# A hybrid decoder step on one core: value products one page at a time, probability turns two pages later, gate weights from ScalarE's queue, 4 key and 5 value page buffers, a combine step spread between gate products

## The reference

```
z = rmsnorm(x) @ w_in                       # q, k, v of two attentions, two gates
o_fox = softmax(q k^T/8 + c_q - c_k) v      # forgetting attention; samples: 2048 past keys in 16 pages
o_dil = sum_g softmax_g(lse_g) * o_g        # three dilated windows, mixed by their log-sum-exp
y = (sigmoid(gate_fox)*(o_fox @ w_br_fox) + sigmoid(gate_dil)*(o_dil @ w_br_dil)) @ w_mix_out
x = x + y ; then cross attention into 256 memory rows ; then a gated MLP with a convolution
```

## Time and profile before

| | us |
|---|---|
| median of 3 runs | 3113.7 (3109.15 to 3117.74) |
| the profiled execution | 3115.95 |
| its span | 3114.1 |
| PE busy | 2959.3 (95%) |
| DVE busy | 848.8 (27%) |
| ACT busy | 565.3 (18%) |
| mean granted clock of PE | 0.972 |

### The profile page before, as it was taken

One profiled execution on the slowest core, in us unless ns is written; L12 is line 12 of the kernel. 1 busy time (PEld: TensorE's weight loads), 2 busy tenths in 40 slices (PEclk: granted clock), 3 DMA queues, 4 the chain that ended last, 5 costly groups with the idle time before them and its releaser, 6 DMA issues.

```text
span 3114.1 us, 35981 instructions
## 1 busy us (share of the span) xinstructions
PE 2959.3 (95%) x13892; PEld 1862.2 (60%) x13892; DVE 848.8 (27%) x2145; ACT 565.3 (18%) x1247; POOL 135.3 (4%) x251
## 2 busy tenths in 40 slices
PE   8999999999789888889899999999999999999998
PEld 6655556776435444456544566446666666678887
DVE  2154543222532222223221023332222222210002
ACT  2233222212101111111100111322212212210001
POOL 0000001011001111000000000000000000000000
PEclk9999999999969999999999999999999999999999
DMA  4000111010136657545501301323433431121101
GB/s 170 20 11 8 52 45 53 11 47 15 30 105 174 199 159 206 181 155 163 204 27 54 135 28 48 128 66 116 146 118 120 152 118 42 29 86 38 38 1 58
DMA packets 195295, 276.95 MB, mean 89 GB/s; under 512 B 19741, under 2 KB 135406, under 8 KB 194086
## 3 DMA queue, kind: packets, MB, share of 16 engines
q1 hardware_dynamic: 177302, 210.83, 21.4%
q10 hardware_dynamic: 1504, 44.29, 3.7%
q0 software_dynamic: 16320, 19.52, 2.4%
HBM read 255.09 MB, written 58.90 MB: 101 GB/s over the span
## 4 chain that ended last, share of the span: by engine, by line
PE 82%; SPq 8%; DMA 4%; issue 3%; DVE 2%; ACT 0%; POOL 0%; DVEq 0%; POOLq 0%; ACTq 0%
PE psum L2240 21%; PE psum L2384 11%; PE psum L920 10%; PE psum L1870 8%; PE psum L1785 6%; PE psum L2005 4%; SPq L1399 3%; PE psum L677 3%; PE psum L693 3%; PE psum L1220 2%; DMA arena<-in_cache_fox_kv 2%; PE psum L1793 2%; PE psum L507 2%; PE psum L1236 2%; PE psum L1979 2%
## 5 line engine op out<-in xcount | busy, mean ns | idle before, releaser
L2240 PE MATMUL psum<-arena 128*128 128x288 f32 (+1 forms) x2112 | 645.9, 469 | 0.0
L2240 PEld LDWEIGHTS psum<-arena 128*128 128x128 f32 x2112 | 402.0, 190 | 243.5 <-issue 169.6
L2384 PE MATMUL psum<-arena 128*128 128x256 f32 (+1 forms) x1584 | 345.5, 381 | 0.7 <-DMA arena<-in_w_down 0.7
L920 PE MATMUL psum<-arena 128*128 128x512 f32 (+3 forms) x864 | 332.3, 515 | 1.4 <-ACT arena L560 1.4
L2384 PEld LDWEIGHTS psum<-arena 128*128 128x128 f32 (+1 forms) x1584 | 292.2, 185 | 53.5 <-issue 3.6
L1785 PE MATMUL psum<-arena 128*128 128x368 f32 (+1 forms) x768 | 310.8, 501 | 0.0
L1870 PE MATMUL psum<-arena 128*128 128x512 f32 (+1 forms) x576 | 266.0, 598 | 0.8 <-issue 0.8
L920 PEld LDWEIGHTS psum<-arena 128*128 128x128 f32 (+1 forms) x864 | 195.5, 262 | 70.2 <-issue 42.1
L1220 PEld LDWEIGHTS psum<-arena 128*128 128x128 f32 x848 | 107.4, 145 | 109.4 <-DMA arena<-in_cache_fox_kv 47.9
L1220 PE MATMUL psum<-arena 128*128 128x128 f32 x848 | 134.1, 282 | 35.7 <-DMA arena<-in_cache_fox_kv 35.2
L1785 PEld LDWEIGHTS psum<-arena 128*128 128x128 f32 x768 | 124.6, 195 | 63.6 <-issue 44.1
(11 more groups left out here) (207 smaller groups left out, 2630.7 us busy)
## 6 DMA issues: line engine op xcount, KB each, us to landing
arena<-in_cache_fox_kv SPq DMA_DIRECT2D x256, 256.0 KB, 3.1
out_win_s<-in_cache_win_kv ACTq DMA_DIRECT2D x8, 4080.0 KB, 15.3
arena<-in_w_up SPq DMA_DIRECT2D x44, 512.0 KB, 4.5
arena<-in_cache_win_kv SPq DMA_DIRECT2D x16, 1024.0 KB, 6.9
arena<-in_cache_mem_kv SPq DMA_DIRECT2D x16, 1024.0 KB, 6.0
arena<-in_w_down SPq DMA_DIRECT2D x4, 2816.0 KB, 9.9
arena<-in_w_in SPq DMA_DIRECT2D x9, 1024.0 KB, 7.8
arena<-in_x_prompt SPq DMA_DIRECT2D x16, 512.0 KB, 6.6
```

The lines of the kernel that those rows point to most:

```text
L920: last = pe.matmul(banks[c0 // 512][0:r, 0:cw], xn_tile(k, g, t), wD[g][:, k, c0:c0 + cw], start=(k == 0), stop=(k == KD - 1))
L2240: last = pe.matmul(banks[(u % 2) * 4 + x][:, 0:cw], wu[u % 3][:, k, :], xnT[:, k, c0:c0 + cw], start=(k == 0), stop=(k == KD - 1))
L2384: last = pe.matmul(banks[u % 2][0:r, 0:256], hT(f)[:, t * P:t * P + r], wd[q % 2][:, f, :], start=(f == 0), stop=(f == NF - 1))
```

## The change

Five things are changed; what is computed stays the same.

1. The schedule of the page attention is written with explicit offsets: the P of a sample come 2 to 6 pages into the next sample (before: 0, 2, 3, 4, 5), each V is one page (16 parts instead of 9; the last takes the new tokens too) at offsets 4 to 18, and O comes at 20. A V waits only for the group of probabilities that it reads, and P is copied as soon as the V that reads its old content is done.
2. Nine page buffers are split 4 for keys and 5 for values (before 3 and 6).
3. The gate weights are issued by ACT (`gates_load_act`) instead of SP, into two buffers instead of three.
4. In `PLAN`, `combine` has 84 units instead of 34, with more points at which gate products can stand between its pieces; `fox` has 360 (before 300), `dil` 192 (125), and `gb` 438 (258).
5. The window attention's mask and its 24 small loads of new keys are issued a quarter into `fox` (`dilprep_sp`), and the memory norm stands 14 units after the start of `mix`.

```diff
-    combine=(778, 812), ga=(715, 1010), gb=(1010, 1268), foxprep=(767, 777), fox=(814, 1114), dilprep=(1115, 1117),
-    dil=(1117, 1242), gs=(1270, 1284), mix=(1284, 1410), nm=(1286, 1300), n2=(1300, 1426),
+    combine=(776, 860), ga=(715, 1010), gb=(1010, 1448), foxprep=(765, 775), fox=(862, 1222), dilprep=(1226, 1228),
+    dil=(1230, 1422), gs=(1450, 1464), mix=(1464, 1590), nm=(1478, 1490), n2=(1494, 1620),
...
 def combine_dve(dve):
...
             for g in range(NG):
                 dve.tensor_tensor(ls[g], ls[g], nm[g], ALU.mult).then_inc(cb["weighted"], 1)
+            yield now(0.57)
...
+            yield now(0.61)
             dve.wait_ge(cb["own"], 4)
             dve.reciprocal(dn, dn).then_inc(cb["own"], 1)
+            yield now(0.68)
...
 def paged(...):
+            tails = [(nt * (b + 1) + off, b, x, kind, q) for b in range(NB) for x, (kind, q, off) in enumerate(tail_at)]
...
+                sched += [(kind, bb, q) for slot, bb, _, kind, q in tails if slot == n]
...
 def pages_pe(pe, a, k_ready, v_ready):
...
-                    if i == 0:
-                        pe.wait_ge(s["p_kept"], z["p_kept"] + (b + 1) * a["nps"])
-                        if b:
-                            pe.wait_ge(s["scaled"], z["scaled"] + b)
+                    pe.wait_ge(s["p_kept"], z["p_kept"] + b * a["nps"] + a["p_for_part"][i] + 1)
+                    if i == 0 and b:
+                        pe.wait_ge(s["scaled"], z["scaled"] + b)
...
-        NVR = 6
+        NKR, NVR = 4, 5
...
 def foxk_sp(sp):
-                if m >= 3:
-                    sp.wait_ge(*nth(pg_fox, "turned", m - 2))
+                if m >= NKR:
+                    sp.wait_ge(*nth(pg_fox, "turned", m - NKR + 1))
...
+        fox_split = [[p] for p in range(NPG - 1)] + [[NPG - 1, NPG]]
+        fox_tail = [("P", q, 2 + q) for q in range(5)] + [("V", p, 4 + 15 * p // 16) for p in range(NPG)] + [("O", 0, 20)]
...
+        def dilprep_sp(sp):
+            yield at("fox")(0.25)
+            sp.wait_ge(cb["second"], 4)
+            for g in range(NG):
+                win_stored(sp, g)
+            sp.dma_start(tab_d, TAB["win_sample"]).then_inc(dn2["in"], 16)
+            for g, (w, _) in enumerate(WINS):
+                new = O[f"win{w}_s"][0, :, w - NS:w].rearrange("b s v h d -> b s v (h d)")
+                for bb in range(NB):
+                    sp.dma_start(kn_d[bb * NS:(bb + 1) * NS, g, :], new[bb, :, 0, :]).then_inc(dn2["in"], 16)
...
-        def gates_sp(sp):
+        def gates_load_act(act):
...
-                yield gate_due(3 * (q - 2)) if q >= 3 else gate_due(0) - 30 + q
+                yield gate_due(3 * (q - 1)) if q >= 2 else gate_due(0) - 30 + q
...
+                if q >= 2:
+                    act.wait_ge(gt["computed"], 3 * (q - 1))
+                s = gt[f"w_in{q % 2}"]
+                act.dma_start(wg[q % 2][:, 0:8, :], w_in[:, :, col + m * P:col + (m + 1) * P]).then_inc(s, 16)
+                act.dma_start(wg[q % 2][:, 8:8 + kn, :], w_br[:, :, m * P:(m + 1) * P]).then_inc(s, 16)
```

More of the change, by code:

```diff
@@ L1070, in combine_pe @@
             for g in range(NG):
-                yield now(0.15 * g)
+                yield now(0.12 * g)
                 if g == 0:
@@ L1174, in paged @@
-            tail = [("P", q) for q in range(nps)] + [("V", q) for q in range(v_parts)] + [("O", 0)]
-            for b in range(NB):
-                for i in range(nt):
-                    sched.append(("T", b, i))
-                    more = bool(scores)
-                    while more:
-                        sched.append(scores.pop(0))
-                        if sched[-1][0] == "M":
-                            tails += [(k, sched[-1][1], q) for k, q in tail]
-                        more = bool(scores) and (scores[0][0] == "M" or gl[scores[0][2]]["turned"] is None)
-                    if tails and i in tail_turns:
-                        sched.append(tails.pop(0))
+            sched, scores = [], []
@@ new lines, in paged @@
+            tails = [(nt * (b + 1) + off, b, x, kind, q) for b in range(NB) for x, (kind, q, off) in enumerate(tail_at)]
+            tails.sort()
+            for n in range(max(t[0] for t in tails) + 1):
+                b, i = n // nt, n % nt
+                if b < NB:
+                    sched.append(("T", b, i))
+                more = bool(scores)
+                while more:
+                    sched.append(scores.pop(0))
+                    more = bool(scores) and (scores[0][0] == "M" or gl[scores[0][2]]["turned"] is None)
+                sched += [(kind, bb, q) for slot, bb, _, kind, q in tails if slot == n]
+                if b < NB:
@@ L1186, in paged @@
                     scores += [("S", b, x) for x in range(len(gl))
                                if gl[x]["turned"] == i + 1 or (i == 0 and gl[x]["turned"] is None)]
-                scores.append(("M", b, 0))
-            sched += scores + tails + [(k, NB - 1, q) for k, q in tail]
+                    if i == nt - 1:
+                        scores.append(("M", b, 0))
+            assert not scores
+            v_parts = len(v_split)
+            part_of = {x: i for i, part in enumerate(v_split) for x in part}
@@ new lines, in group_of @@
+            def group_of(x):
+                return min(x // per_p, nps - 1)
+            tail_waits, last_tail = {}, None
+            for e in sched:
+                if e[0] in "PO":
+                    tail_waits[e] = last_tail
+                    last_tail = ("p_kept", e[1] * nps + e[2] + 1) if e[0] == "P" else ("taken", e[1] + 1)
+            p_for_part = [max(group_of(x) for x in part) for part in v_split]
+            part_for_p = [max(part_of[x] for x in part_of if group_of(x) == q) for q in range(nps)]
@@ L1264, in pages_pe @@
                     pe.wait_ge(s["scaled"], z["scaled"] + b + 1)
+                    if a["tail_waits"][(what, b, i)] is not None:
+                        pe.wait_ge(*nth(a, *a["tail_waits"][(what, b, i)]))
                     for x in range(a["o_blocks"]):
@@ L1368, in build @@
         bias_f = take(1024, f0 + 6656).rearrange("p (g c) -> p g c", g=2)
-        v_fox = take(NVR * 512, f0 + 7680).rearrange("p (n c) -> p n c", n=NVR)
+        pages = [take(512, f0 + a) for a in (0, 512, 1024, 7680, 8192, 8704, 9216, 9728, 10240)]
+        k_fox, v_fox = pages[0:NKR], pages[NKR:]
         PT_f = take((NPG + 1) * 64, f0 + 10752).rearrange("p (n j c) -> p n j c", j=4, c=16)
@@ L1469, in fox_turns @@
         def fox_turns(b):
-            return [dict(blocks=[k_fox[:, (b * NPG + p) % 3, j * P:(j + 1) * P] for j in range(4)],
+            return [dict(blocks=[k_fox[(b * NPG + p) % NKR][:, j * P:(j + 1) * P] for j in range(4)],
                          dst=lambda kt, p=p: kt[:, :, (p % 4) * P:(p % 4 + 1) * P],
@@ L1737, in build @@
         sig = [take(368, X0 - KD * TOK - 736 + 368 * i) for i in range(2)]
-        wg = [take(1536, f0 + 28160 + 1536 * i).rearrange("p (k n) -> p k n", n=P) for i in range(3)]
+        wg = [take(1536, f0 + 29696 + 1536 * i).rearrange("p (k n) -> p k n", n=P) for i in range(2)]
         sgs = take(2 * KD * SM, f0 + 32768).rearrange("p (a m c) -> p a m c", a=2, m=KD)
         w_bs = take(6 * D, f0 + 8192).rearrange("p (k n) -> p k n", k=6)
-        gt = sems("gates", "w_in0 w_in1 w_in2 ws_in computed opened branched gated merged s_computed s_gated s_merged")
+        gt = sems("gates", "w_in0 w_in1 ws_in computed opened branched gated merged s_computed s_gated s_merged")
         w_bf = I["w_br_fox"][0].rearrange("(k p) n -> p k n", p=P)
```

113 lines of the change are left out of this document (50 added, 63 removed).

## The result

The kernel after takes 3018.8 us (median of 4 runs, 3012.9 to 3026.9), the kernel before 3115.7 us in the same comparison (4 runs, 3109.2 to 3119.5): 0.97 times the time, 95% interval 0.9683 to 0.9716. The forecast was 3022 us.

What follows compares the result with a forecast made beforehand. PE, busy 95% of the span, bounds the kernel; only its waits and half-clock time can be won. Stage terms sum to -92.5 us, taking the profiled 3115.95 us to 3021 to 3023, forecast 3022 us; range 2988 to 3072.

Steps and rivals of the forecast that it cites:

- signs of being right: Trace signs: 5 to 8 us idle before L1090, intervals about 50 then 41 us, no waits for ACT or memory transposes.
- Combine: From first L1079 to first T: 79 us instead of 74.3, so +4.6 us, with more gate products placed there.
- Fox: The page attention stage: 375 us against 433.3, so -58.2 us.
- 24.9 us of work: PE's work in fox's first interval, first T to first P, forecast to take 31 us instead of 44.9.
- small losses: In fox, 11 us added: 4 for small-load issues, 4 for O and P on one bank, 3 for weights on ACT.
- Handover: Between fox and dil: small loads have landed long before, 5.5 us instead of 18, so -12.5 us.
- dil: Stage after the handover, PE nearly always busy: 11 gate products fewer at 0.70 us, so -7.7 us.
- Behind dil: After dil, before mix: 10 products fewer, 6.0 us less, plus 1.3 for later branch weights of L1803: -4.7 us.
- Pages at 191 GB/s: Rival, chance 0.18: in fox pages cannot come faster, late samples take 48.4 us each; 3054 us with the tail.
- Only the page stage pays: Rival, chance 0.08: the handover and mix only exchange one wait for another; 3047 us.
- The clock: Rival, chance 0.06: waits in fox's late samples bring PE's clock down and keep it down; 3160 us.
- Everything closes: Rival, chance 0.11: late samples at 37 us, no half clock in combine, small losses 3 us; 2994 us.

Runs made afterwards that it cites:

- the last kernel: Kernel after, with separate branch-weight waits, page number read before the buffer wait, small loads spread singly, and DVE's combine steps closer together: 3006.3 us, 0.9659.
- the split wait: Kernel after, with the samples' branch products waiting for each of their two weights where used, instead of both at the start: 3015.5 us, 0.9694.
- the run with both handovers back: Kernel after, with mask and 24 small loads again issued after the page attention and the memory norm 2 units after the output product's start: 3038.9 us, 0.9763.

## Why the prediction was right, step by step

The total is 3 us off, within the spread of the runs, and the likeliest case was the one that came. The mechanisms held in the main: all the signs of being right were seen. Two sizes did not hold, `fox` by 10.0 us and what comes behind the last O of `dil` by 10.1 us. They have opposite signs, and that they cancel is luck.

- *Combine*: forecast +4.6 with 6.6 us idle and 4.5 us of half clock. Measured +4.7 with 5.48 us idle and 32.6 us instead of 24.9 + 1.7 for the rest, so more clock was lost (6 us) and less waiting. The price of the clock was near, its cause was not: I put it down to the idle stretch, and the last kernel, with none there, has 0.84 against 0.82. The stage was priced by following DVE's list piece by piece, and this held to 1.5 us. The same rest took 32.1 to 35.9 us in the nine other kernels with this `combine`, so a few us here are chance.
- *Fox*: -68.2 instead of -58.2. The first interval was 38.1 us, not 31. "24.9 us of work" has 16 T and 19 gate products, those of the first sample; but the first P now comes two pages into the second, and up to it PE does 18 T and 26 gate products. It is busy for 32.3 us there (31.2 in the kernel with constant page numbers). The wait for keys is 6.1 us, just what I had allowed. The next three intervals, 46, 50.2 and 49.4 us, measured 48.6, 52.6 and 45.8, right in sum (147.0 against 145.6), with the 3.4 us of the small loads in them. The late four, forecast as 41 each, took 41.1, 40.5, 38.9 and 37.4, 6 us less in all: PE is busy for 148 us of them, near the 4 x 36.6 forecast, and idles 9.5 us where I had allowed 17.6. The tail was 1.7 us shorter, with 12 gate products in it instead of 16. The 11 us of small losses, set as a sum of their own, do not come on top: the gate weights on ACT cost nothing that can be measured, and for O and the P behind it on one bank no run has a number. So +7.1, +1.4, -6.1, -1.7 and -11: -10.3. The term that was most mis-sized is waiting.
- *What makes up the 68*: by the two last rows of the table by stretch, PE idles 41.5 us less and is busy 26.7 us less. Of the latter 27 gate products at 0.7 us are 19 (counted and priced, not measured); the other 8 fit a clock of 1.00 instead of 0.93, which no run isolates. Undone alone, four key buffers are worth 18 us, values evenly and by single pages 20 (13 and 7, with the reserve on value buffers above), the later P 11, and the small loads in SP's list cost 3 to 6. Such terms overlap and need not add up.
- *What bounds fox*: that SP's reading of the page number is the limit, and not the transfers, was argued from 3.35 us for three pages. Constants in its place show how far it holds. In the kernel before they take 41.5 us out of 433, but 19.7 of 35.2 us of key waits stay, so the reading was the largest cause and not the only one. In the kernel after they take out 17.4 us and nearly all key waits.
- *Handover* (-13.7) and *dil* (-8.4): right to 1.2 us.
- *Behind dil*: the step that went wrong. "10 x 0.60 = 6.0 less", with 1.3 us for the weights. The weights did come late by about that, 1.75 us of idle instead of 0.72. What I did not price was the clock behind so short a wait: the 48 products of 64 columns took 18.21 instead of 10.90 us, 7.3 us, and the first products of `mix` 2.1 more (the x40 of L1895, 19.48 us against 17.41 with the split wait). So +2.3 instead of -4.7, and -9.7 instead of -12.8 behind it. This is chance in part: in six of ten profiles with such a wait the same products ran at full clock. The 10.85 us of waiting for the memory rows are gone, but part of that is the slow L1828 too: where it ran at full clock, 0 to 1.8 us of the wait are left, except in the run that puts it back.
- *Pages at 191 GB/s*: refuted by the late intervals, 244 GB/s in one of them. Its figure was an average that includes stretches in which SP issued no value pages. *Only the page stage pays*: refuted by the run with both handovers back. *The clock*: the late intervals held 1.00, with 2.0 to 2.9 us idle in each, against 6 of 27 us in the stretch at 0.75. *Everything closes* (2994) did not come. That the kernel with constant page numbers has 2994.3 us is a coincidence: its late samples agree, at 35 to 39 us against 37, its other stages do not.

## What to carry to other kernels

When a transfer's place is read from memory by the issuing engine, price each issue with that reading: here 1.1 us a page against 0.5 without it, and this, more than the bytes, set the pace. Spread the wants of such a queue evenly, one value page to one key page, and give the buffers to the operand that the engine waits for: the two were worth about the same here, 20 and 18 us. When an event moves to a later place in a schedule, count again what stands ahead of it: 7 us of the first interval were missed so. Undo each part of a combined change alone and read the stage, not the total: 6.7 us lost in one stage were hidden by a clock that did not fall in another.

## What the runs showed of the hardware

Behind a wait of less than 2 us, with small products following, the granted clock fell in some executions and not in others. In front of L1828 (48 products of 64 columns, each as two instructions) PE stands idle for 1.6 to 1.8 us in ten kernels of the same code at that place. In four profiles the products then took 18 to 20 us (granted clock 0.57 in the one shown), in six 10.9 us (1.00). The idle was 1.69 to 1.84 us in the four and 1.64 to 1.83 in the six, so its length does not decide. With 0.7 to 0.8 us idle it was 10.9 us in four of four, too few to tell from chance. The two outcomes lie 7 to 8 us apart, a quarter of a per cent of this kernel, as much as several of the edits above are worth.

In the spreading part of `combine` the clock was 0.56 over 30 us after 19.9 us of idle, 0.82 over 32.6 us after 5.5 us, and 0.84 over 32.0 us after none. Long idle ahead costs clock there, but taking the last 5.5 us of it away gave back next to nothing.
